# A third chunk by halves, x's squares in fours, and the decoder step's jobs placed anew

## The reference, cut to what matters

```python
h = rmsnorm(x, g_mix);  proj = h @ w_in          # 1024 x 2048: u | q | k | v, 512 columns each
q, k = rope(q), rope(k)                          # 8 heads of 64
pool_out = pool_mix(u, state)                    # causal means over 2, 4, 8, 16 rows, minus the row, times w_pool
attn = attention(q, k, v)                        # prompt: causal over 256 keys; decoding: 256 cached keys + its own
x = x + concat(pool_out, attn) @ w_out
mk, mv = rmsnorm(mem, g_mem) @ w_ck, ... @ w_cv   # 256 rows of memory, for the prompt
x = x + cross_attend(rmsnorm(x, g_cross), mk, mv) # 4 heads of 256; w_cq and w_co
x = x + square(relu(rmsnorm(x, g_mlp) @ w_up)) @ w_down    # width 4096
y = rmsnorm(x, g_final)
```

## Time and profile before

| | us |
|---|---|
| median of 3 runs (lowest, highest) | 425.88 (425.37, 426.50) |
| the profiled execution | 427.42 |
| its span, first to last instruction of the program | 425.6 |
| TensorE busy in it | 415.0 (98%) |
| TensorE's weight loads busy | 389.2 (91%) |
| VectorE busy | 255.8 (60%) |
| ScalarE busy | 225.2 (53%) |
| GpSimd busy | 38.7 (9%) |
| share of the chain of waits on TensorE | 88% |

### The profile page before, as it was taken

One profiled execution on the slowest core, in us unless ns is written; L12 is line 12 of the kernel. 1 busy time (PEld: TensorE's weight loads), 2 busy tenths in 40 slices (PEclk: granted clock), 3 DMA queues, 4 the chain that ended last, 5 costly groups with the idle time before them and its releaser, 6 DMA issues.

```text
span 425.6 us, 8409 instructions
## 1 busy us (share of the span) xinstructions
PE 415.0 (98%) x3372; PEld 389.2 (91%) x3372; DVE 255.8 (60%) x372; ACT 225.2 (53%) x395; POOL 38.7 (9%) x48
## 2 busy tenths in 40 slices
PE   8799989999999999999999999999999999999995
PEld 8799978986869999867799999999999999999994
DVE  4789999693345687542359767667667534454302
ACT  6846766654463674424347566665655433453213
POOL 1602026000000220000003100000000000010010
PEclk9899999999999999999999999999999999999999
DMA  7998097948996965898627635555555655546002
GB/s 279 411 379 267 31 366 220 346 168 338 335 380 223 411 256 228 322 367 314 245 100 226 256 110 196 195 176 168 199 197 180 206 169 189 187 157 174 2 2 102
DMA packets 36969, 96.60 MB, mean 227 GB/s; under 512 B 4282, under 2 KB 12858, under 8 KB 36794
## 3 DMA queue, kind: packets, MB, share of 16 engines
q1 hardware_dynamic: 34962, 92.50, 61.3%
q10 hardware_dynamic: 1968, 3.55, 2.3%
HBM read 91.73 MB, written 4.54 MB: 226 GB/s over the span
## 4 chain that ended last, share of the span: by engine, by line
PE 88%; DVE 5%; DMA 3%; ACT 1%; SPq 1%; issue 1%; DVEq 0%; ACTq 0%
PE psum L1069 74%; PE psum L803 5%; PE psum L1014 2%; PE psum L928 2%; PE psum L915 2%; DMA raw<-in_w_ck 2%; DMA raw<-in_w_in 1%; DVE w_lo L1342 1%; ACT w_hi L1089 1%; PE psum L861 1%; PE psum L921 0%; DVE act_lo L1346 0%; DVE soft L1460 0%; PE psum L899 0%; PE psum L834 0%
## 5 line engine op out<-in xcount | busy, mean ns | idle before, releaser
L1342 DVE TENSOR_TENSOR w_lo<-raw,w_hi 128x1024 fp32r<-128x1024 f32 x68 | 84.5, 1250 | 65.3 <-ACT w_hi L1089 64.8
L1089 ACT ACTIVATE w_hi<-raw 128x1024 fp32r<-128x1024 f32 (+1 forms) x72 | 73.8, 1031 | 64.1 <-PE psum L1069 47.1
L1069 PE MATMUL psum<-mix_hi,w_hi 128*128 128x264 f32 (+1 forms) x288 | 82.7, 287 | 0.0
L1069 PE MATMUL psum<-mix_lo,w_hi 128*128 128x264 f32 (+1 forms) x288 | 81.6, 283 | 0.0
L1069 PE MATMUL psum<-mix_hi,w_lo 128*128 128x264 f32 (+1 forms) x288 | 81.6, 283 | 0.0
L1069 PE MATMUL psum<-act_hi,w_hi 128*128 128x264 f32 x240 | 69.9, 291 | 2.2 <-DVE act_lo L1346 2.2
L1069 PE MATMUL psum<-act_lo,w_hi 128*128 128x264 f32 x240 | 69.0, 287 | 0.0
L1069 PE MATMUL psum<-act_hi,w_lo 128*128 128x264 f32 x240 | 68.9, 287 | 0.0
L1621 POOL TENSOR_TENSOR ssq<-ssq,sq 128x264 f32<-128x264 f32 (+1 forms) x34 | 30.0, 883 | 330.8 <-ACT sq L1110 328.7
L1069 PEld LDWEIGHTS psum<-mix_hi,w_hi 128*128 128x128 f32 x288 | 54.3, 189 | 0.5 <-issue 0.4
L1069 PEld LDWEIGHTS psum<-mix_lo,w_hi 128*128 128x128 f32 x288 | 54.2, 188 | 0.1
(11 more groups left out here) (196 smaller groups left out, 800.2 us busy)
## 6 DMA issues: line engine op xcount, KB each, us to landing
raw<-in_w_down SPq DMA_DIRECT2D x20, 512.0 KB, 4.1
raw<-in_w_up SPq DMA_DIRECT2D x18, 512.0 KB, 4.1
raw_more<-in_w_up SPq DMA_DIRECT2D x14, 512.0 KB, 3.8
stage<-in_mem_v SPq DMA_DIRECT2D x12, 512.0 KB, 5.7
raw_more<-in_w_down SPq DMA_DIRECT2D x12, 512.0 KB, 4.2
keysT<-in_cache_k SPq DMA_DIRECT2D x16, 256.0 KB, 5.1
stage<-in_cache_v SPq DMA_DIRECT2D x16, 256.0 KB, 5.3
keysT<-in_mem_k SPq DMA_DIRECT2D x8, 512.0 KB, 6.6
```

The lines of the kernel that those rows point to most:

```text
L1069: mm = pe.matmul(out, a, b, start=first and m == 0, stop=end_ and m == 2)
L1089: return nc.scalar.activation(out, in_, ACT.Copy, scale=scale)
L1342: V.tensor_tensor(lo_of(c), raw_of(c), hi_of(c).bitcast(F32), ALU.subtract).then_inc(w_lo_ready, 1)
```

## The change

w_in's third chunk (PARTED = 3) is loaded, split and multiplied by halves too; in these chunks the pass lo x hi now stands before hi x lo. The gains and x are one array: the first load brings the gains and tile 0, then come tiles 1, 2 and 3 singly, and 4-5 and 6-7 in pairs. x's squares are two ScalarE operations of four tiles each (jobs "square_x"), and VectorE adds the eight squares in three pairwise additions (job "sum_x") in place of GpSimd; they lie in the cached keys' buffer, so loads of K wait for the sum. The statistics of x follow chunk 4. In "S", VectorE adds the mask and takes the maximum in one operation (tensor_tensor_reduce), for the first 128 columns and the other 256, and the maxima are negated afterwards. "m_tile" is cut into ScalarE's part and VectorE's ("m_lo"). "norm" gets a semaphore of its own, and a branch for ScalarE that is not used (SCALED_BY_ACT is empty). Nearly all jobs up to chunk 31 and the loads up to chunk 33 get new places.

```diff
-PARTED = 2
-STAT_X = 3
+PARTED = 3
+STAT_X = 4
...
-    put(3, ("stat", "x"), ("split",))
-    put(4, ("tables",))
+    put(0, ("square_x", 1), ("square_x", 0))
+    put(1, ("sum_x",), ("split",))
+    put(2, ("split",))
+    put(4, ("stat", "x"), ("tables",), ("split",), ("turn", 0))
-    put(6, ("turn", 0), ("split",))
-    put(7, ("turn", 2))
-    put(8, ("m_tile", 1), ("m_tile", 2))
-    put(9, ("S", 0), ("S", 1), ("S", 2), ("S", 3), ("m_tile", 3), ("turn", 1), ("turn", 3))
-    put(10, ("exp", 0), ("exp", 1))
-    put(11, ("exp", 2))
-    put(12, ("exp", 3), ("k_out",), ("norm", 0), ("m_tile", 4))
-    put(13, ("qblock",), ("m_tile", 5))
-    put(14, ("P_T", 0), ("P_T", 1), ("P_T", 2), ("P_T", 3))
-    put(15, ("S", 4), ("S", 5), ("S", 6), ("S", 7), ("m_tile", 6), ("cS", 0), ("m_tile", 7))
-    put(16, ("stat", "m"), ("v_nat", 0))
-    put(18, ("stat_col", "m"), ("exp", 4))
-    put(19, ("exp", 5))
-    put(20, ("differences",))
-    put(21, ("exp", 6), ("v_nat", 1), ("exp", 7), ("norm", 1))
-    put(23, ("cS", 1), ("O", 0), ("P_T", 4))
-    put(24, ("split",), ("P_T", 5))
-    put(25, ("cP_T",), ("split",))
-    put(26, ("O", 1), ("cO", 0))
-    put(27, ("P_T", 6))
-    put(29, ("P_T", 7), ("pool", 0), ("pool", 1), ("pool", 2))
-    put(30, ("O", 2), ("cO", 1))
-    put(31, ("pool", 3), ("c_attn",), ("O", 3))
+    put(7, ("turn", 2), ("split",), ("m_tile", 1), ("m_tile", 2))
+    put(8, ("m_tile", 3), ("m_lo", 0), ("m_lo", 1), ("m_lo", 2), ("S", 0), ("S", 1), ("S", 2), ("S", 3))
+    put(9, ("m_tile", 4), ("turn", 1), ("exp", 0), ("turn", 3))
+    put(10, ("qblock",), ("exp", 1))
+    put(11, ("exp", 2), ("exp", 3), ("split",))
+    put(12, ("k_out",), ("v_nat", 0))
+    put(13, ("v_nat", 1), ("norm", 0), ("split",))
+    put(14, ("m_tile", 5), ("P_T", 0), ("m_lo", 3), ("m_lo", 4), ("P_T", 1), ("P_T", 2))
+    put(15, ("m_tile", 6), ("m_lo", 5), ("P_T", 3), ("m_tile", 7), ("S", 4), ("S", 5), ("S", 6), ("S", 7), ("m_lo", 6), ("cS", 0), ("O", 0))
+    put(16, ("split",), ("stat", "m"), ("exp", 4))
+    put(17, ("m_lo", 7), ("split",))
+    put(18, ("exp", 5), ("stat_col", "m"), ("exp", 6))
+    put(19, ("exp", 7), ("split",), ("O", 1), ("norm", 1))
+    put(21, ("split",))
+    put(22, ("cS", 1))
+    put(23, ("differences",), ("P_T", 4))
+    put(24, ("split",), ("P_T", 5), ("cP_T",))
+    put(25, ("P_T", 6), ("P_T", 7))
+    put(26, ("cO", 0), ("split",), ("O", 2), ("pool", 0))
+    put(27, ("pool", 1))
+    put(29, ("split",))
+    put(30, ("pool", 2))
+    put(31, ("cO", 1), ("O", 3), ("pool", 3), ("c_attn",))
...
-UNITS = [(("m", i), ("m_tile", 4 * i), ("m_tile", 4 * i + 3)) for i in range(2)]
+UNITS = [(("m", i), ("m_tile", 4 * i), ("m_lo", 4 * i + 3)) for i in range(2)]
...
-    4: ["tables"],
-    6: [("m", 1)],
-    7: [("m", 0), "constants"],
-    12: [("K", 3)],
-    14: [("V", 2)],
-    15: [("V", 0), ("K", 0)],
-    16: [("K", 1)],
-    17: ["state"],
-    18: [("wpool",)],
-    20: [("K", 2), ("V", 1)],
-    22: [("K", 6)],
-    23: [("K", 7)],
-    24: [("K", 4), ("K", 5)],
-    26: [("V", 3)],
-    28: [("mK", 0, 1)],
-    29: [("V", 4)],
-    31: [("mK", 0, 0), ("V", 7)],
-    33: [("V", 5), ("V", 6)],
-    34: [("mK", 0, 2)],
+    6: ["tables", ("m", 0)],
+    8: ["constants"],
+    10: [("V", 2)],
+    11: [("V", 0)],
+    12: [("K", 1)],
+    15: [("K", 3), ("m", 1)],
+    16: [("V", 3), ("K", 0)],
+    18: [("V", 1), ("K", 2)],
+    22: [("K", 4), "state", ("wpool",)],
+    23: [("K", 5), ("K", 7)],
+    25: [("K", 6)],
+    27: [("V", 4)],
+    29: [("mK", 0, 1)],
+    30: [("mK", 0, 2)],
+    31: [("V", 7)],
+    32: [("V", 5)],
+    33: [("mK", 0, 0), ("V", 6)],
...
+        x_squares = keysT.rearrange("p s k n -> p (s k n)")[:, 0:KT * T].rearrange("p (k t) -> p k t", k=KT)
...
                 elif what == "K":
+                    sp.wait_ge(x_summed, 1)
...
-            load_x(1)
+            load_x(2, 1)
             load_part(1, 1)
-            for i in range(2, 4):
-                if i < RAW:
-                    load_weights(i)
-                load_x(i)
+            load_x(3, 1)
+            load_part(2, 0)
+            load_part(2, 1)
+            load_x(4, CK)
+            load_x(6, CK)
...
-                    pe.wait_ge(sq_added, (KT - 1) * (m + 1))
+                    if i[0] == "x":
+                        pe.wait_ge(x_summed, 1)
+                    else:
+                        pe.wait_ge(sq_added, (KT - 1) * m)
...
+                        pe.wait_ge(first_lo_ready, k + kk + 1)
+                        for x, bank in enumerate(banks):
+                            pe.matmul(psum[:, bank, 0:T], lo[:, kk, x * P:(x + 1) * P], act_hi[:, k + kk, :], start=False, stop=False)
                         pe.wait_ge(stream_lo, k + kk + 1)
                         for x, bank in enumerate(banks):
-                            pe.matmul(psum[:, bank, 0:T], hi[:, kk, x * P:(x + 1) * P], act_lo[:, k + kk, :], start=False, stop=False)
-                        pe.wait_ge(first_lo_ready, k + kk + 1)
-                        for x, bank in enumerate(banks):
-                            mm = pe.matmul(psum[:, bank, 0:T], lo[:, kk, x * P:(x + 1) * P], act_hi[:, k + kk, :], start=False, stop=False)
+                            mm = pe.matmul(psum[:, bank, 0:T], hi[:, kk, x * P:(x + 1) * P], act_lo[:, k + kk, :], start=False, stop=False)
...
+                if what == "square_x":
+                    x = slice(4 * i[0], 4 * i[0] + 4)
+                    nc.scalar.activation(x_squares[:, x, :], xT[:, x, :], ACT.Square).then_inc(x_squared, 1)
+                    return
...
-            square("x", 0, xT[:, 0, :], T)
-            split_hi(2)
-            round_x(2)
-            square("x", 1, xT[:, 1, :], T)
-            square("x", 2, xT[:, 2, :], T)
             round_x(3)
                 split_hi(s)
-            for k in range(3, KT):
-                square("x", k, xT[:, k, :], T)
...
-                    V.tensor_tensor(soft[:, slot, 0:3 * P], B[:, 0:3 * P], causal, ALU.add).then_inc(bank_free[PLACE[job][0]], 1)
+                    V.tensor_tensor_reduce(soft[:, slot, 0:P], B[:, 0:P], causal[:, 0:P], 1.0, NEG, ALU.add, ALU.max, stats[:, slot, 0:1])
+                    V.tensor_tensor_reduce(soft[:, slot, P:3 * P], B[:, P:3 * P], causal[:, P:3 * P], 1.0, NEG, ALU.add, ALU.max, stats[:, slot, 1:2]).then_inc(bank_free[PLACE[job][0]], 1)
-                        V.tensor_reduce(stats[:, 0:4, 0:1], soft[:, 0:4, 0:P], AX_X, ALU.max, negate=True)
-                        V.tensor_reduce(stats[:, 0:4, 1:2], soft[:, 0:4, P:3 * P], AX_X, ALU.max, negate=True).then_inc(max_ready, 1)
+                        V.tensor_scalar(stats[:, 0:4, 0:2], stats[:, 0:4, 0:2], -1.0, None, ALU.mult).then_inc(max_ready, 1)
...
+                if what == "sum_x":
+                    dve.wait_ge(x_squared, 2)
+                    then(V.tensor_tensor(x_squares[:, 0:4, :], x_squares[:, 0:4, :], x_squares[:, 4:8, :], ALU.add))
+                    then(V.tensor_tensor(x_squares[:, 0:2, :], x_squares[:, 0:2, :], x_squares[:, 2:4, :], ALU.add))
+                    V.tensor_tensor(ssq[:, 0, :], x_squares[:, 0, :], x_squares[:, 1, :], ALU.add).then_inc(x_summed, 1)
...
-            split_lo(2)
...
-            add_squares("x")
```

More of the change, by code:

```diff
@@ L52 @@
 STATE = max(WINDOWS) - 1
+GAINS = 6 * KT
 FF = 4 * D
@@ L206 @@
 OPENER = {closer: opener for opener, closer in CLOSER.items()}
-NO_PRODUCTS = ("m_tile", "differences", "tables", "turn", "qblock", "k_out", "exp", "norm", "split")
+SCALED_BY_ACT = ()
+NO_PRODUCTS = ("m_tile", "m_lo", "differences", "square_x", "sum_x", "tables", "turn", "qblock", "k_out", "exp", "norm", "split")
 def plan_banks():
@@ L275 @@
 MAXED = {j: i for i, j in enumerate(j for j in SOFT if j[0] != "S" or j[1] % 4 == 3)}
+SOFT_READY = {j: i + 1 for i, j in enumerate(j for j in SOFT if j[0] != "S")}
 SOFT_T = turns(("P_T", "xP_T"))
@@ L704, in load @@
                     sp.wait_ge(parts_used, PARTS[prior] + 1)
-                elif prior[0] == "m_tile":
+                elif prior[0] == "m_lo":
                     sp.wait_ge(stream_lo, STREAM["m"] + prior[1] + 1)
@@ L1103, in square @@
                 m = NORM[norm]
-                added = (KT - 1) * m + max(k - SQ_SLOTS, 0)
+                added = (KT - 1) * (m - 1) + max(k - SQ_SLOTS, 0)
                 if added > 0:
@@ L1210, in run @@
                     last.then_inc(exp_ready, 1)
+                    return
+                if what == "norm" and i[0] in SCALED_BY_ACT:
+                    act.wait_ge(heads_inverted, i[0] + 1)
+                    for h in range(4 * i[0], 4 * i[0] + 4):
+                        slot = SOFT["S", h] % SOFTS
+                        for x, (a, b) in enumerate(((0, P), (P, 3 * P))):
+                            last = copy(soft[:, slot, a:b], soft[:, slot, a:b], stats[:, slot, 4 + x:5 + x])
+                        last.then_inc(heads_ready, 1)
                     return
@@ L1490, in run @@
                 what, *i = job
```

(13 more changed lines are left out.)

54 lines of the change are left out of this document (28 added, 26 removed).

## The result

The changed kernel takes 422.64 us (median of 12 executions, 422.15 to 425.09); the kernel before, on the same chip, 426.22 (12, 425.37 to 428.70). The ratio is 0.992, 95% interval 0.9906 to 0.9935: 3.6 us faster. The forecast was 421.1, with a range of 419.8 to 424.6.

A forecast was written before the change was run, and what follows sets the result against it. TensorE, busy nearly all of the span, bounds the kernel. 3.6 + 1.8 - 0.3 - 0.3 = 4.8 us off the profiled 427.42 gives 422.6, less 1.54 for the median 421.1; range 419.8 to 424.6.

The forecast's parts named there:

- The sum against its own execution: All terms over the span: 3.6 + 1.8 - 0.3 - 0.3 = 4.8 us won, taking the profiled 427.42 to 422.6.
- First product: x's first tile lands earlier, so TensorE's first product starts near 5.15 in place of 5.80: 0.65 us won (0 to 0.8).
- Third and fourth chunk: Third chunk by halves: TensorE stands 1.0 us where it stood 2.25, no half clock, fourth done at 17.9; 3.6 won by here.
- Squares and statistics: x's squares and sum around chunks 4 and 5: sum at 19.2, at the tightest 1.2 us of cover, cost 0.
- Scores 0 to 3: After chunk 8: TensorE there at 33.3, VectorE's turn 2 done at 33.2, no slack; stall of 0.3 us (0 to 1.0).
- Maxima: Mask and maximum in one operation: 2.7 us per four heads in place of 3.8, 1.1 of VectorE's won.
- Transposes of head 0 and scores 4 to 7: Scaling done at 52.7, TensorE there at 53.1: waits of 1.47 and 0.34 us go, with 0.3 counted as left.
- The step that failed: From profiled execution to median: 422.6 less the 1.54 us by which the earlier median lay below its profiled execution, 421.1.
- rival B: VectorE late between 33 and 53, by maxima at 4.3 or turn 2: 1.1 to 2.8 more, 422.2 to 423.9; chance 0.15.
- A: The fourth chunk's wait exceeds 1.0 us and half clock follows: 1.7 + 0.3 more, 423.1; chance 0.14.
- C: Slower than before: new maxima at 0.8 us each or more delay head 0's transposes, clock falls; 429.3 at 1.2 each; chance 0.04.
- E: Early gain given back in jobs of chunks 15 to 31: 3 to 5 us added, 424.1 to 426.1; chance 0.10.

The follow-up runs named there:

- the repeat: The kernel before, run again with no edit: 426.26 us, ratio 1.0002; its profiled execution took 425.91 us.
- The two kernels with the scores later: Changed kernel with the memory's load and scores of heads 0 to 3 one chunk later, 421.42 us; the same with the third chunk whole, 422.26 us.
- the GpSimd run: Changed kernel with the three additions of x's squares on GpSimd in place of VectorE: 425.18 us, ratio 0.997.

## Why the prediction was right, and where it was not

**The sum against its own execution.** It had 4.8 us of span; the two profiles show 5.5. The steps below measure 3.97 - 0.43 - 0.60 + 1.81 = 4.75, and chunk 32 indeed starts 4.76 us earlier (126.47 to 121.71); the other 0.7 lies behind it. That 4.8 came true to a tenth is luck: 0.4 and 0.3 more were won, at the fourth chunk and the transposes, and 0.4 and 0.3 more lost, at the statistics and the scores. By steps:
- First product: forecast 5.15, came at 5.50. The first rounded operands were there 0.45 us later than taken, since the 256 KB of w_in landed at 4.30 and not 3.76: ScalarE idled 1.14 for it, 0.61 before. This goes with the change: its first w_hi starts at 4.27 to 4.47 in all nine traces of kernels with the new loads, at 3.49 to 3.79 in the four without. Of the 0.65 counted, 0.06 is left after four tiles (11.80 against 11.85): the first four matmuls took 0.97 us for 0.72, since the clock rose only after they had begun. In the warm-up before them the matmuls started 0.21 us apart to the end; in the kernel before the last ones were already 0.11 apart.
- Third and fourth chunk: forecast a stand of 1.0 and the end at 17.9; it came at 17.73 with no stand. The fourth chunk's w_hi started at 12.20, not 12.65 (the forecast's own terms make 12.8 or more), since x's tile 4 was rounded by 10.55 and not 10.95. And the halves ended at 14.71, not 14.0, so w_lo (1.23, as taken) was just in time: two errors made the stand vanish, one of them TensorE's own lateness. Won by here 3.97 for the 3.6 forecast, of which the run without the halves leaves them 0.9.
- Squares and statistics: the prices held (1.02 each for the squares, 2.4 for the additions, sum at 18.8 for 19.2), "cost 0" did not: 0.43. The step counted the sum and w_lo but not the copies of q out of the statistics' bank, which stood behind a late w_hi. The load of the memory, the edit's own move, made it late: taking it out of the way removed the wait.
- Scores 0 to 3: counted 0.3, was 0.60, inside the 0 to 1.0 given. VectorE's sum began with the reciprocal at 22.7; it began at 23.39, behind the late statistics. And it took turn 2 without GpSimd beside it; the last operation then took 1.14 and not 0.71. TensorE came at 33.9 and not 33.3, which hides half of this.
- Maxima: 2.6 for the 2.7 taken. The Trainium skill's section on two Vector instructions with no wait between them (VectorE: DVE Perf Modes) is borne out in its structure: each operation is followed by a DVE_READ_ACCUMULATOR2_ANT. But the read takes 0.07 to 0.08 us and overlaps its operation's end, not the 0.18 of ScalarE's, so the 1.4 us priced from that did not come.
- Transposes of head 0 and scores 4 to 7: no wait for either. The residue of 0.3 did not come, but by TensorE's delays: VectorE ended the scaling at 53.43 for the 52.7 forecast, TensorE came at 54.51 for 53.1, and on time it would have stood some 0.5 us (an estimate). The maxima alone took 1.1 us off the kernel before, and without them the other edits left no wait at P_T either: most of the 1.5 us was covered twice.

**The step that failed** is the last, and by it the 422.64 lies above the forecast's own range of 420.0 to 422.4, at a time that the prediction gave to rival B: "The median before, 425.88, is 1.54 below that execution: 421.1." A gain that lies partly in what made the execution slow can't be taken off a median that has none of it. The profiled execution had 1.72 us of half clock and 0.6 us more stand than the repeat at 425.91. From that repeat the same steps give: fourth chunk 19.63 to 17.73, 1.9; statistics 0.54 to 0.43, 0.1; scores -0.6; transposes and second scores 1.47 + 0.13 = 1.6. That is 3.0. The spans are 424.1 and 420.1. Chunk 32 starts 3.3 us earlier (124.99 to 121.71), and 0.6 of the rest lies in the jobs behind chunk 47, the same 198 matmuls at full clock in both:

```profile
173.47:196.79 23.32, 23.32 (x198) 17.07 (x197) 10.25 (x26) 8.34 (x23) 0.00 (x0) 1.00 0.90 348
```

```profile
170.18:192.91 22.73, 22.73 (x198) 17.17 (x197) 10.25 (x26) 8.35 (x23) 0.00 (x0) 1.00 0.93 349
```

(the kernel before repeated, then the changed one). The two kernels with the scores later, alike from chunk 15 on, differ there by 0.4 as well (22.76 and 23.17), so this is taken for the scatter of executions, not for the change. Last, the time outside the span: 1.8 us in the runs of the kernel before, 2.1 in those of the changed one (medians), 2.0 to 2.15 in each of the eight made from the changed one, 1.8 in the two made from the kernel before. Four of span less 0.3 is 3.7; the two medians (426.2 and 422.6) give 3.6. The prediction had no term for it. What in the change adds it is open, but the 2.0 to 2.15 stay without the halves, without the new maxima, with the sum on GpSimd and with the old jobs, so it is none of these; no run takes out the squares in fours or the new loads of x.

**Rivals.** A did not come: no stand, so no half clock, in the trace. What it says of the clock stood: a stand of 3.67 us was followed by half clock, for 1.5 to 1.7 us lost as priced, and one of 2.25 in the GpSimd run too, there for some 3.4; stands of 1.8, 1.65 and 1.47 left the clock at 1.00. B's mechanism stood in small part: the scores waited 0.3 us more than counted. That the measured time is near B's 422.2 is no sign of B, for its 1.1 to 2.8 us of lateness did not come. C fell with 0.28 and 0.41 us for the operation. E fell: no job between chunks 15 and 31 costs TensorE a wait that the list shows.

**Shares.** They don't add, since most of them are bounded by the same waits. By ratios, in us: placement 1.8 and the sum on VectorE and not GpSimd 2.1, both clear of noise; maxima 0.9 added to the kernel before, clear, and 0.8 taken from the changed one, not clear; halves -0.7, +0.6 and -0.5 in the three settings, none of them clear. The last run, with neither halves nor placement, is still 2.1 us below the kernel before; beside the maxima that is x's squares and the new loads of x, which no run tried by themselves.

## What to carry to other kernels

Before a gain is taken off a median, look whether the profiled execution is the median's kind: a stretch at half clock that it has and the median lacks can't be won there. Time won early on the bounding engine is only kept if the next things that it meets (here a PSUM bank's copies, then kT) move forward too; list every producer of the next job, its buffer's last reader included, with the queue that each stands in. An edit that looked like the main one (the halves, which win 0.9 us at the fourth chunk) can be worth nothing at the end: take each part out of the finished kernel before it is given a share. And when a job moves, ask what its other engines will run beside: the memory's additions on GpSimd slowed the operation that the next job waited for.

## What the runs showed that was not expected

Executions of one kernel split where a stand of some 2 us comes early on: the kernel before stood 2.25 us and lost 1.72 more at clock 0.51 in one profile, stood 1.65 and lost nothing in the next; with the sum on GpSimd they spread over 4.4 us.

VectorE and GpSimd slow each other. The two operations of turn 2 that write kT took 0.71 us in 17 of the 26 cases in the thirteen traces, and 1.1 to 1.2 in the nine that began while an addition of GpSimd was under way. It goes both ways: GpSimd's additions of x's squares took 2.47, 2.19 and 1.60 us for 1056, 528 and 264 columns (VectorE's took 1.26, 0.71 and 0.43), while the kernel before has two of 264 columns in 1.63 us together; and the w_lo that ran beside the first two of them took 2.65 us for the usual 1.22. A kernel that keeps the memory's additions away from turn 2 was not run.

Two executions of the changed kernel (424.86 and 425.09, clock 0.994 and 0.995) show a lower clock though its trace has no stand of over 0.6 us after the start; no run was made to find why.
